# Six RMS normalisations in a three-block transformer kernel: rows scaled on VectorE and transposed, in place of products with a diagonal matrix

## The chip, the cores and the metric

The kernel runs on one NeuronCore of one Trainium2 chip. The metric is the device time of one execution in microseconds; the kernel before takes 2475.67 us (median of three runs, 2475.46 to 2476.18).

## The reference

Three blocks in a row work on one sequence of 256 tokens with 1024 channels, all in float32. Each block has two layers or one, and every layer is a mixer (attention, convolution or a recurrence) or a feed-forward part behind an RMS norm:

```python
def rms_norm(x, g, eps=1e-6):
    xf = x.astype(jnp.float32)
    y = xf * lax.rsqrt(jnp.mean(xf * xf, axis=-1, keepdims=True) + eps)
    return (y * g.astype(jnp.float32)).astype(x.dtype)

# block 1, layer l = 0, 1
h = rms_norm(x, norm1_g[l]) * (1.0 + scale1) + shift1        # norms 0 and 2
...
x = x + (1.0 + gate1) * mixed
h2 = rms_norm(x, norm2_g[l]) * (1.0 + scale2) + shift2       # norms 1 and 3
x = x + (1.0 + gate2) * ((jax.nn.silu(f_gate) * f_up) @ w_ffn_out[l])
# block 2 has one layer: its norm is norm 4
# block 3, layer l = 0, 1
h = rms_norm_3(x, norm_mix[l])                               # norms 5 and 7
x = x + hybrid_mixer(h, ...)
h = rms_norm_3(x, norm_ffn[l])                               # norms 6 and 8
x = x + swiglu(h, ...) if l % 2 == 0 else x + moe_swiglu(h, ...)   # eight experts, top k
```

## The kernel before

The tokens lie in two tiles of 128 partitions (t = 0, 1), the stream `x` is [128, 2, 1024] in SBUF. Every weight is loaded in chunks of 128 x 2048 into six `raw` buffers by SyncE. ScalarE rounds a chunk to `head` (L693), VectorE makes `rest = raw - head` (L1147, `make_rest`), and TensorE does each product in three matmuls of the float32r parts (`three`, L2019 to L2021). The activations go the same way: `hT` (channels on partitions) is split into `hTh` by ScalarE (L710) and `hTl` by VectorE (L1275, `rest_turned`). Each engine runs a program written out by hand; the order of the work is the order of the calls in it, and `feed` puts the chunk work (L693, L1147) between the rest.

The nine norms are numbered 0 to 8 in the order in which they run. A norm must turn `x` (tokens on partitions) into `hT` (channels on partitions), scaled by 1/rms of each token. For each tile t:

- ScalarE squares and sums (L722) and takes the root (L751 or L743);
- VectorE, in `scale_diagonal`, takes the reciprocal (L1252) and makes a diagonal matrix `diag[:, t, :] = ident * r` (L1254);
- TensorE, in `turn_norm`, waits for `diag_ready` and makes eight products of a 128 x 128 block of `x` with `diag` (L2142), which transpose and scale at once, in two halves of four, each with a step on `norm_turned`;
- VectorE, in `evac_turned`, brings each half from PSUM to `hT` with the gain (and, in blocks 1 and 2, the shift) per channel: four operations of 128 x 128 (L1266) where there is a shift, one of 128 x 512 (L1262) where there is none. ScalarE and VectorE then split it (L710, L1275).

Norms 1, 3, 6 and 8 follow an output product of a mixer (`norm_of_product`): TensorE, in `linear_by_tiles`, does all of tile 0, half of tile 1, then `turn_norm(n, 0, ...)`, then the other half of tile 1. VectorE adds tile 0 to the stream, scales, evacuates, and then waits for the last product of tile 1 to add it (L1288/L1290 or L1285). Behind the second `scale_diagonal` it makes the rest of one more weight chunk (L1147) before it evacuates tile 1, except in norm 8. TensorE meanwhile begins the feed-forward part on tile 0 in `ffn`: the first chunk for tile 0, then `turn_norm(n, 1, x)`, the second chunk for tile 0 (which needs that L1147), then both for tile 1.

Norms 2 and 7 (and 4) follow a feed-forward part (`norm_of_ffn`): TensorE has nothing between the last product and the next mixer but the two `turn_norm`, and the mixer's first product needs `hTl` of three half tiles. Norm 8 is that of the mixture of experts; there VectorE also makes the normalised rows `xn = x * r * gain` (L1321, L1337), which the gather of the experts' tokens multiplies (L2411), and the router's logits (L2387) need `hT`.

`xn` is [128, 2, 1024] too. Norms 4 and 5 have it as the source of their products, since there x times a gain is normalised a second time.

## Time and profile before

| | |
|---|---|
| median of 3 runs | 2475.67 us |
| the profiled execution's own time | 2475.45 us |
| its span in the trace | 2473.6 us |
| TensorE busy | 2363.7 us (96%) |
| VectorE busy | 1942.6 us (79%) |
| ScalarE busy | 1419.4 us (57%) |
| mean granted TensorE clock | 0.984 |
| mean DMA rate | 264 GB/s |

Busy times are sums over the span. A matmul's duration in the trace holds its way through the pipeline, so that matmuls in a row overlap; the distance from start to start tells the rate. Times in the views of the timeline and of the stretches are microseconds from the span's start. "Idle before, releaser" is how long an engine stood before an instruction and what ended that.

### The profile page before, as it was taken

What the parts mean: (1) busy time and instruction counts of PE and PEld (TensorE: products, weight loads), DVE (VectorE), ACT (ScalarE), POOL (GpSimd) and SP (SyncE); (2) the same over time, 40 slices, a digit from 0 to 9 for tenths busy, and PEclk for the clock granted to TensorE, in tenths of its full rate; (3) what the DMA queues carried; (4) which work ended last, traced back from release to release, by engine and by line L of the source; (5) the groups of instructions that cost most, each with busy time, mean ns of one, the idle gap of its engine ahead of it and who ended that gap; (6) DMA issues with size and microseconds to landing.
All of it is one profiled execution on the core that took longest, in us unless ns stands there. A gap on an engine that the chain in (4) does not pass through costs nothing.

```text
span 2473.6 us, 29836 instructions
## 1 busy us (share of the span) xinstructions
PE 2363.7 (96%) x11895; PEld 1979.3 (80%) x11895; DVE 1942.6 (79%) x1866; ACT 1419.4 (57%) x1410; POOL 17.4 (1%) x33
## 2 busy tenths in 40 slices
PE   4988999998999899899999989999999999999998
PEld 4866788867888798798888978888888888888886
DVE  6998878787797656675445769898989898989897
ACT  2654433546443454455334547777777777777776
POOL 0000000000000000000000000000000000000000
PEclk9998999999999999899999999999999999999999
DMA  9556889444598445445555439999999999999996
GB/s 339 189 181 240 304 294 347 158 139 142 188 340 298 148 158 180 133 165 186 188 195 181 155 131 360 360 363 351 358 351 365 352 361 353 360 354 361 348 365 217
DMA packets 434768, 652.93 MB, mean 264 GB/s; under 512 B 20144, under 2 KB 323888, under 8 KB 434624
## 3 DMA queue, kind: packets, MB, share of 16 engines
q1 hardware_dynamic: 432592, 644.63, 75.3%
q0 software_dynamic: 2032, 6.33, 0.8%
q8 instruction: 97, 1.59, 0.3%
q14 instruction: 47, 0.39, 0.0%
HBM read 649.82 MB, written 1.05 MB: 263 GB/s over the span
## 4 chain that ended last, share of the span: by engine, by line
PE 89%; DVE 7%; ACT 2%; issue 1%; DMA 1%; SPq 0%; ACTq 0%; DVEq 0%
PE pair L2019 27%; PE pair L2021 26%; PE pair L2020 26%; PE pair L2054 2%; PE tb L2230 2%; DVE rest L1147 1%; PE pair L2411 1%; DVE aw L1516 1%; PE pair L2142 1%; DMA raw<-in_ada_w 1%; PE tb L2097 1%; DVE gat L1166 1%; DVE hT L1266 1%; ACT aw L722 0%; PE pair L2155 0%
## 5 line engine op out<-in xcount | busy, mean ns | idle before, releaser
L1147 DVE TENSOR_TENSOR rest<-raw,head 128x2048 fp32r<-128x2048 f32 x544 | 1245.0, 2291 | 295.6 <-ACT head L693 279.9
L693 ACT ACTIVATE head<-raw 128x2048 fp32r<-128x2048 f32 x544 | 1039.3, 1912 | 325.1 <-PE pair L2021 294.2
L2019 PE MATMUL pair<-head,hTh 128*128 128x512 f32 x1864 | 744.2, 399 | 6.3 <-issue 3.0
L2021 PE MATMUL pair<-head,hTl 128*128 128x512 f32 x1864 | 728.3, 391 | 0.0
L2020 PE MATMUL pair<-rest,hTh 128*128 128x512 f32 x1864 | 727.3, 390 | 0.0
L2019 PEld LDWEIGHTS pair<-head,hTh 128*128 128x128 f32 x1864 | 350.8, 188 | 79.6 <-issue 9.1
L2021 PEld LDWEIGHTS pair<-head,hTl 128*128 128x128 f32 x1864 | 350.3, 188 | 74.4
L2020 PEld LDWEIGHTS pair<-rest,hTh 128*128 128x128 f32 x1864 | 351.1, 188 | 69.4 <-issue 1.2
L2019 PE MATMUL pair<-head,aTh 128*128 128x512 f32 x776 | 308.4, 397 | 4.0 <-issue 2.9
L2020 PE MATMUL pair<-rest,aTh 128*128 128x512 f32 x776 | 303.7, 391 | 0.0
L2021 PE MATMUL pair<-head,aTl 128*128 128x512 f32 x776 | 303.7, 391 | 0.0
L2019 PE MATMUL pair<-hTh,head 128*128 128x256 f32 x736 | 211.3, 287 | 15.4 <-issue 7.2
L2020 PE MATMUL pair<-hTl,head 128*128 128x256 f32 x736 | 209.9, 285 | 0.0
L2021 PE MATMUL pair<-hTh,rest 128*128 128x256 f32 x736 | 209.8, 285 | 0.0
L928 ACT ACTIVATE aTh<-tb 128x256 fp32r<-128x256 f32 (+1 forms) x145 | 62.8, 433 | 231.3 <-PE tb L2230 231.3
L2019 PEld LDWEIGHTS pair<-head,aTh 128*128 128x128 f32 x776 | 146.6, 189 | 38.5 <-issue 9.1
L2021 PEld LDWEIGHTS pair<-head,aTl 128*128 128x128 f32 x776 | 146.6, 189 | 31.2
L2020 PEld LDWEIGHTS pair<-rest,aTh 128*128 128x128 f32 x776 | 146.8, 189 | 30.5 <-issue 1.0
L924 ACT ACTIVATE qkv<-pair 128x256 f32<-128x256 f32 (+1 forms) x148 | 64.6, 436 | 174.8 <-PE pair L2021 174.8
L2019 PEld LDWEIGHTS pair<-hTh,head 128*128 128x128 f32 x736 | 143.0, 194 | 17.0 <-issue 8.8
L2020 PEld LDWEIGHTS pair<-hTl,head 128*128 128x128 f32 x736 | 143.1, 194 | 0.1
L2021 PEld LDWEIGHTS pair<-hTh,rest 128*128 128x128 f32 x736 | 142.9, 194 | 0.0
(302 smaller groups left out, 1637.8 us busy)
## 6 DMA issues: line engine op xcount, KB each, us to landing
raw<-in_moe_w_gate SPq DMA_DIRECT2D x224, 512.0 KB, 5.2
raw<-in_moe_w_up SPq DMA_DIRECT2D x224, 512.0 KB, 7.2
raw<-in_moe_w_down SPq DMA_DIRECT2D x224, 512.0 KB, 5.6
raw<-in_w_in SPq DMA_DIRECT2D x152, 512.0 KB, 4.6
raw<-in_ada_w SPq DMA_DIRECT2D x96, 512.0 KB, 5.5
raw<-in_w_ffn_in SPq DMA_DIRECT2D x88, 512.0 KB, 5.3
raw<-in_w_ffn_out SPq DMA_DIRECT2D x44, 512.0 KB, 5.4
raw<-in_w_out SPq DMA_DIRECT2D x40, 512.0 KB, 4.3
```

The costliest lines, as they stand in the source:

```text
L693: act.activation(head[:, c.split, :], raw[:, c.raw, :], ACT.Copy).then_inc(heads_done, 1)
L924: act.activation(sg[:, 0:nt, :], src, ACT.Silu).then_inc(sem("silu_ready"), 1)
L928: act.activation(aTh[:, :, 0:nt * P], tb[0][:, :].rearrange("p (k s) -> p k s", k=2)[:, :, 0:nt * P], ACT.Copy).then_inc(ath_ready, 1)
L1147: dve.tensor_tensor(rest[:, c.split, :], raw[:, c.raw, :], head[:, c.split, :].bitcast(F32), ALU.subtract).then_inc(rests_done, 1)
L1166: ins = dve.scalar_tensor_tensor(out=acc, in0=src, scalar=c_, in1=acc, op0=ALU.mult, op1=ALU.add)
L1266: ins = dve.tensor_scalar(hT[:, k, toks], ps[:, i, :], scale[:, k:k + 1], shift[:, k:k + 1], ALU.mult, ALU.add)
L1516: did(dve.scalar_tensor_tensor(out=conv[:, g, :], in0=upad[:, g, k:k + S], scalar=w_, in1=conv[:, g, :], op0=ALU.mult, op1=ALU.add))
L2019: pe.matmul(out_, lh, rh, start=start, stop=False, skip_group_check=True)
L2020: pe.matmul(out_, lh, rl, start=False, stop=False, skip_group_check=True)
L2021: return pe.matmul(out_, ll, rh, start=False, stop=stop, skip_group_check=True)
L2054: ins = pe.matmul(ps[:, t, :], hT[:, kk, toks], raw[:, c.raw, wcols], start=first, stop=last, skip_group_check=True)
L2230: ins = pe.transpose(tb[0][:, k * S + t * P:k * S + (t + 1) * P], act_[:, t, k * P:(k + 1) * P], ident)
```

## The change

The norms 1, 2, 3, 6, 7 and 8 (`TURNED`) no longer use the diagonal matrix; 0, 4 and 5 (`DIAGONAL`) do so as before. In the six, VectorE multiplies the rows of `x` by the reciprocal, in two halves of 128 x 512, into `xn`, with a step on `rows_scaled` for each half, and TensorE transposes the blocks of `xn` against the identity. In norm 8 the scaling takes the gain in as well, so that it also makes the rows for the gather; the evacuation there is then a plain copy, and TensorE's wait for `xn_ready` ahead of the gather goes.

```diff
+        DIAGONAL, TURNED = (0, 4, 5), (1, 2, 3, 6, 7, 8)
...
-            def scale_diagonal(t, squared=None):
+            def scale_rows(n, t, squared=None):
...
                 did(dve.reciprocal(r, r))
                 now()
-                dve.tensor_scalar(diag[:, t, :], ident, r, None, ALU.mult).then_inc(sem("diag_ready"), 1)
+                if n in DIAGONAL:
+                    dve.tensor_scalar(diag[:, t, :], ident, r, None, ALU.mult).then_inc(sem("diag_ready"), 1)
+                    return
+                for half in range(2):
+                    cols = slice(half * NT, (half + 1) * NT)
+                    if n == 8:
+                        dve.wait_ge(sem("gain_landed"), 16)
+                        ins = dve.scalar_tensor_tensor(out=xn[:, t, cols], in0=x[:, t, cols], scalar=r, in1=gain[:, cols],
+                                                       op0=ALU.mult, op1=ALU.mult)
+                    else:
+                        ins = dve.tensor_scalar(xn[:, t, cols], x[:, t, cols], r, None, ALU.mult)
+                    ins.then_inc(sem("rows_scaled"), 1)
 
             def evac_turned(n, t, half, scale, shift):
...
+                if n == 8:
+                    dve.tensor_copy(hT[:, ks, toks], ps).then_inc(sem("hT_ready"), 1)
+                    return
...
-                scale_diagonal(0, None if g is None else base + 6)
+                scale_rows(n, 0, None if g is None else base + 6)
                 tally["squared"] += 4 * per
-                if n == 8:
-                    dve.wait_ge(sem("gain_landed"), 16)
-                    dve.scalar_tensor_tensor(out=xn[:, 0, :], in0=x[:, 0, :], scalar=rstd[:, 0:1], in1=gain,
-                                             op0=ALU.mult, op1=ALU.mult).then_inc(sem("xn_ready"), 1)
...
-                scale_diagonal(1, None if g is None else base + 8)
-                if n == 8:
-                    dve.scalar_tensor_tensor(out=xn[:, 1, :], in0=x[:, 1, :], scalar=rstd[:, 1:2], in1=gain,
-                                             op0=ALU.mult, op1=ALU.mult).then_inc(sem("xn_ready"), 1)
+                scale_rows(n, 1, None if g is None else base + 8)
...
             def turn_norm(n, t, src):
 
                 free(f"norm{n}.{t}")
-                pe.wait_ge(sem("diag_ready"), 2 * n + t + 1)
+                if n in DIAGONAL:
+                    pe.wait_ge(sem("diag_ready"), 2 * DIAGONAL.index(n) + t + 1)
                 for half in range(2):
+                    if n in TURNED:
+                        pe.wait_ge(sem("rows_scaled"), 4 * TURNED.index(n) + 2 * t + half + 1)
                     for i in range(4):
                         cols = slice((4 * half + i) * P, (4 * half + i + 1) * P)
+                        if n in TURNED:
+                            ins = pe.transpose(bank(f"norm{n}.{t}")[:, half, i * P:(i + 1) * P], xn[:, t, cols], ident)
+                            continue
                         ins = pe.matmul(bank(f"norm{n}.{t}")[:, half, i * P:(i + 1) * P], src[:, t, cols], diag[:, t, :], start=True, stop=True)
                     ins.then_inc(sem("norm_turned"), 1)
...
-            pe.wait_ge(sem("xn_ready"), 2)
```

Nothing else moves. Three places on VectorE show it. The first is norm 2, between the first addition of tile 1 and the end of the norm; before (L1252 the reciprocal, L1254 the diagonal, L1266 the evacuation, L1275 the rest of `hT`):

```order
L1252 RECIPROCAL sm<-sm 128x1
L1254 TENSOR_SCALAR diag<-cst,sm 128x128
L1288 TENSOR_TENSOR gat<-pair,gbc 128x512
L1290 TENSOR_TENSOR x<-x,gat 128x512
L1235 TENSOR_SCALAR sm<-sm 128x1
L1266 TENSOR_SCALAR hT<-pair,sm 128x128 x4
L1252 RECIPROCAL sm<-sm 128x1
L1254 TENSOR_SCALAR diag<-cst,sm 128x128
L1266 TENSOR_SCALAR hT<-pair,sm 128x128 x8
L1275 TENSOR_TENSOR hTl<-hT,hTh 128x4x128 x3
```

The same place now (L1265 is the scaling, L1281 the evacuation, L1290 the rest of `hT`):

```order
L1253 RECIPROCAL sm<-sm 128x1
L1265 TENSOR_SCALAR xn<-x,sm 128x512 x2
L1303 TENSOR_TENSOR gat<-pair,gbc 128x512
L1305 TENSOR_TENSOR x<-x,gat 128x512
L1236 TENSOR_SCALAR sm<-sm 128x1
L1281 TENSOR_SCALAR hT<-pair,sm 128x128 x4
L1253 RECIPROCAL sm<-sm 128x1
L1265 TENSOR_SCALAR xn<-x,sm 128x512 x2
L1281 TENSOR_SCALAR hT<-pair,sm 128x128 x8
L1290 TENSOR_TENSOR hTl<-hT,hTh 128x4x128 x3
```

Two operations of 128 x 512 stand where one of 128 x 128 stood, ahead of the second addition and ahead of the evacuation of the second half tile.

The second place is tile 1 of norm 3, now (norms 1 and 6 read alike; before, L1254 stood in the place of L1265, and L1147 is L1148 here):

```order
L1290 TENSOR_TENSOR hTl<-hT,hTh 128x4x128
L1253 RECIPROCAL sm<-sm 128x1
L1265 TENSOR_SCALAR xn<-x,sm 128x512 x2
L1148 TENSOR_TENSOR rest<-raw,head 128x2048
L1281 TENSOR_SCALAR hT<-pair,sm 128x128 x8
```

The rest of the weight chunk stands behind the two scalings.

The third place is tile 1 of norm 8, before:

```order
L1252 RECIPROCAL sm<-sm 128x1
L1254 TENSOR_SCALAR diag<-cst,sm 128x128
L1337 SCALAR_TENSOR_TENSOR xn<-x,sm,gbc 128x1024
L1262 TENSOR_TENSOR hT<-pair,prm 128x4x128 x2
L1851 COPY sm<-tb 128x16
```

and now:

```order
L1253 RECIPROCAL sm<-sm 128x1
L1262 SCALAR_TENSOR_TENSOR xn<-x,sm,gbc 128x512 x2
L1274 COPY hT<-pair 128x4x128 x2
L1859 COPY sm<-tb 128x16
```

The diagonal is gone, and the one operation over 1024 columns is two over 512, which TensorE now waits for.

## Rows read from the trace of the kernel before

**Rows 1.** The page: busy times, and the chain that ended last, by engine.
```profile
PE 2363.7 (96%) x11895; PEld 1979.3 (80%) x11895; DVE 1942.6 (79%) x1866; ACT 1419.4 (57%) x1410; POOL 17.4 (1%) x33
PE 89%; DVE 7%; ACT 2%; issue 1%; DMA 1%; SPq 0%; ACTq 0%; DVEq 0%
```

**Rows 2.** Groups by line: busy us, mean ns | idle before, releaser.
```profile
L2142 PE MATMUL pair<-diag,x 128*128 128x128 f32 x224 | 30.6, 295 | 7.0 <-DVE diag L1254 7.0
...
L1254 DVE TENSOR_SCALAR diag<-cst,sm 128x128 f32<-128x128 f32 x18 | 5.2, 287 | 0.6
...
L1359 DVE TENSOR_SCALAR x<-xn,sm 128x1024 f32<-128x1024 f32 x4 | 2.8, 752 | 0.1
```

**Rows 3.** Timeline, TensorE, a transpose step of the first feed-forward part: start, us.
```profile
267.45 0.60 PE L2230 MATMUL tb<-cst,qkv 128*128 128x128 f32 x4
```

**Rows 4.** Timeline of norm 2: start, us, engine, line [idle before <-releaser].
```profile
447.26 0.29 DVE L1254 TENSOR_SCALAR diag<-cst,sm 128x128 f32<-128x128 f32 x1
...
447.69 2.02 PE L2142 MATMUL pair<-diag,x 128*128 128x128 f32 x16 [0.97 <-DVE diag L1254]
...
448.86 1.37 DVE L1266 TENSOR_SCALAR hT<-pair,sm 128x128 f32<-128x128 f32 x4
...
450.54 2.77 DVE L1266 TENSOR_SCALAR hT<-pair,sm 128x128 f32<-128x128 f32 x8
...
450.77 2.02 PE L2142 MATMUL pair<-diag,x 128*128 128x128 f32 x16 [1.05 <-DVE diag L1254]
...
453.22 1.89 DVE L1275 TENSOR_TENSOR hTl<-hT,hTh 128x512 fp32r<-128x512 f32 x3
...
455.21 0.36 PE L2019 MATMUL pair<-hTh,head 128*128 128x256 f32 x1 [2.42 <-issue]
```

**Rows 5.** Timeline of norm 7: two evacuations, and TensorE's next product.
```profile
1366.42 0.68 DVE L1262 TENSOR_TENSOR hT<-pair,prm 128x512 f32<-128x512 f32 x1
...
1367.82 0.69 DVE L1262 TENSOR_TENSOR hT<-pair,prm 128x512 f32<-128x512 f32 x1 [0.72 <-PE pair L2142]
...
1370.41 0.36 PE L2019 MATMUL pair<-hTh,head 128*128 128x256 f32 x1 [1.74 <-issue]
```

**Rows 6.** Timeline of norm 3: tile 0's products, and tile 1's end.
```profile
630.54 2.02 PE L2142 MATMUL pair<-diag,x 128*128 128x128 f32 x16 [0.55 <-DVE diag L1254]
...
635.34 0.69 DVE L1288 TENSOR_TENSOR gat<-pair,gbc 128x512 f32<-128x512 f32 x1 [0.39 <-PE pair L2021]
...
638.33 2.28 DVE L1147 TENSOR_TENSOR rest<-raw,head 128x2048 fp32r<-128x2048 f32 x1
...
640.76 0.47 PE L2019 MATMUL pair<-head,hTh 128*128 128x512 f32 x1 [0.18 <-DVE rest L1147]
```

**Rows 7.** Timeline of norm 8, VectorE on tile 1.
```profile
1457.26 0.69 DVE L1285 TENSOR_TENSOR x<-x,pair 128x512 f32<-128x512 f32 x1 [2.04 <-PE pair L2021]
...
1459.52 1.28 DVE L1337 SCALAR_TENSOR_TENSOR xn<-x,sm,gbc 128x1024 f32<-128x1024 f32 x1
...
1461.81 0.69 DVE L1262 TENSOR_TENSOR hT<-pair,prm 128x512 f32<-128x512 f32 x1 [0.20 <-PE pair L2142]
```

**Rows 8.** Stretches: us, busy (x) of PE, PEld, DVE, ACT, POOL, granted clock, DMA share, GB/s.
```profile
447.00:455.20 8.20, 4.04 (x32) 3.75 (x33) 8.06 (x24) 3.63 (x8) 0.53 (x1) 1.00 0.17 65
...
1037.70:1041.40 3.70, 3.67 (x17) 3.70 (x18) 2.25 (x5) 1.59 (x3) 1.16 (x2) 0.50 0.34 133
1041.40:1044.00 2.60, 2.60 (x24) 2.60 (x24) 1.88 (x1) 0.69 (x1) 2.31 (x4) 1.00 0.73 214
...
204.00:208.50 4.50, 0.47 (x4) 0.47 (x5) 4.47 (x4) 0.00 (x0) 0.00 (x0) 1.00 1.02 372
208.50:218.80 10.30, 4.73 (x19) 3.94 (x18) 7.65 (x6) 3.70 (x4) 0.00 (x0) 0.50 0.85 294
...
242.70:246.10 3.40, 3.40 (x13) 3.00 (x12) 3.17 (x9) 1.04 (x2) 0.00 (x0) 0.50 0.00 0
```

**Rows 9.** Timeline, TensorE, eight transposes ahead of the first output product.
```profile
215.14 1.97 PE L2132 MATMUL pair<-cst,gat 128*128 128x128 f32 x8 [5.57 <-DVE gat L1601]
```

More of the change, by code:

```diff
@@ L1381, in norm_of_ffn @@
                 add(1, 0)
-                scale_diagonal(0, None if g is None else base + 4)
+                scale_rows(n, 0, None if g is None else base + 4)
                 add(1, 1)
@@ L1385, in norm_of_ffn @@
                 evac_turned(n, 0, 0, scale, shift)
-                scale_diagonal(1, None if g is None else base + 8)
+                scale_rows(n, 1, None if g is None else base + 8)
                 tally["squared"] += 4 * per
@@ L1401, in norm_of_input @@
                 for t in range(T):
-                    scale_diagonal(t)
+                    scale_rows(0, t)
                 tally["squared"] += 2
```

## The prediction, made before the changed kernel had run

> **What bounds the kernel now.** I read the page first: TensorE is busy for 96% of the span and holds 89% of the chain that ended last, VectorE 7% [rows 1]. So time is lost or won only where TensorE stands, or where its own work shrinks. The groups by line come next: the products with the diagonal are records of 295 ns with only 7.0 us of waiting for `diag` in front of them [rows 2]. The timelines of norms 2, 7, 3 and 8 then tell what ends TensorE's pauses around these products, which differs from norm to norm [rows 4 to 7], and the stretches give TensorE's granted clock there [rows 8]. Times are set against the profiled execution, 2475.45 us, which lies 0.22 us under the median of the runs. A difference under 0.2% (5.0 us) is about what a measurement of this kernel can't tell from none.
>
> **The change on TensorE.** A tile's eight products are 16 records in 2.02 us [rows 4]. Without the last record's 0.28 that is 15 steps of 0.116 us, about 0.22 us for a product and 1.8 us for a tile. Four transposes take 0.60 us, the last record 0.27 of it [rows 3]: 0.11 us each, 0.9 us for a tile. Over 12 tiles TensorE is spared 12 x 0.9 = 10.6 us. Few of them lie where TensorE ends a wait.
>
> **The change on VectorE.** The diagonal takes 287 ns over 128 columns, a scaling of the same kind 752 ns over 1024 [rows 2]. On the line between them 512 columns take 0.49 us. Operations in a row overlap by about 0.09 us (the x4 in 1.37 us and the x8 in 2.77 us [rows 4] are 0.35 us apart), so a tile's two scalings hold VectorE for 0.8 us where the diagonal held it for 0.2: **0.6 us more per tile**. The first half is ready 0.2 us later than the diagonal was, the second 0.4 us behind it, which is as long as TensorE needs for the first half's four transposes, 0.44 us.
>
> **Norm 2.** VectorE works without a pause from the first diagonal at 447.26 to the three rests that end at 455.11, and TensorE's next product starts 0.1 us behind them [rows 4]. TensorE's two sets of products end long before they are needed: the second evacuation, of eight, follows on the reciprocal at once. So the saved 1.8 us are worth nothing here, and both scalings lie on the path: 2 x 0.6 = **+1.2 us**. Its bounds are +0.6 (if one of the two finds a gap) and +1.4.
>
> **Norm 7.** It evacuates in one operation per half, so VectorE does have gaps: at 1367.82 it had waited 0.72 us for TensorE's products [rows 5]. I place the new order in time. The first scalings push the addition of tile 1 by 0.6 us, and ScalarE's sum and root with it; the second reciprocal waited for the evacuation until now and so comes only 0.45 later. Its first half is ready 0.65 later than the diagonal was, TensorE then needs 0.44 instead of 0.9 us for it, and the evacuation of tile 1 starts about 0.25 us later. **+0.3 us**, between -0.2 and +1.2 (nothing hidden, as in norm 2).
>
> **Norms 1, 3 and 6.** Tile 0 stands in the stream of products: TensorE waits 0.55 us for the diagonal and then works on it [rows 6]. Now it begins 0.2 later and is done 0.9 earlier: -0.7 us. VectorE was waiting for TensorE's last product of tile 1 when it added it at 635.34 [rows 6], so the gain reaches ScalarE's root and the second reciprocal. There the two scalings take 0.6 us of it back, ahead of the chunk's rest (L1147). TensorE's wait behind the second tile's products ends with that rest, 0.18 us after the products themselves [rows 6]: shorter transposes only make this wait longer. What is left is -0.1 us each, **-0.3 us** in all; bounds -2.1 (the rest not in the way) and +0.3.
>
> **Norm 8.** No chunk's rest stands behind the second scaling. The operation over 1024 columns takes 1.28 us [rows 7], over 512 I take 0.69, as the additions of that width take [rows 7]. From the reciprocal on, the second half is scaled after 1.29 us, transposed after 1.87 and can be evacuated after 2.14; before it was after 2.49 (1461.81 against 1459.32). That is -0.35 us for a tile, and both tiles are on the path, since VectorE waited 2.04 us for TensorE in between [rows 7]: **-0.7 us**, bounds -1.2 and +0.3. The gain is no longer applied in the evacuation; it is a copy of the same width, at the same price. The wait for `xn_ready` that goes had long been satisfied.
>
> Without the clock that makes +1.2 + 0.3 - 0.3 - 0.7 = +0.5 us.
>
> **The clock.** In norm 2 TensorE is busy for 4.04 of 8.20 us, nearly all of it with the diagonal, and the granted clock stays at 1.00, the 2.4 GHz level [rows 8]. With transposes half of that busy time goes and the 8.2 us grow by 1.2 to some 9.4: 1.8 us of transposes in two pieces, and nothing else. The nearest rows: after 4.05 us of idling and the first four transposes, from 204.00 to 208.50, the clock fell to 0.50, the 1.2 GHz level, for 10.3 us [rows 8]. In norm 1 it fell for 3.4 us even with the diagonal there, behind a run of one-column products [rows 8]. So I expect a fall in norm 2, and in norm 7, where the pause is shorter but as empty. What it costs is shown where the same work started at 1037.7 with a low clock: 17 records in 3.70 us, and then, at 1.00, 24 in 2.60 [rows 8]. Half of the 3.7 us is lost: 1.8 us. The clock can also stay low for shorter or longer; 0 and 3.4 us are my bounds for each. Twice 1.8 is **+3.6 us**. TensorE holds 89% of the chain [rows 1], and behind either norm begin the mixer's first products, which wait for nothing else; so I count it in full.
>
> In norms 1, 3 and 6 TensorE's second visit to the norm is now 1.8 us of products and about 0.7 us of idling (some 0.5 before them, as at tile 0, and 0.18 behind [rows 6]). It becomes some 3.1 us with 0.9 us of transposes: it begins 0.7 us earlier and ends 0.1 earlier. That is close to where the clock falls, and I take one fall in the three, at the shortest spell shown: half of 3.4 us [rows 8], **+1.6 us**; bounds 0 and 4.8.
>
> A rule of the Trainium skill speaks to this. TensorE: Matmul & The Clock Gate, Part 4 (PE-mode transpose), says that the full clock "doesn't engage" for transposes, since they don't count as TensorE being busy. By it the three product norms would all fall. The trace agrees only in part: of the eight transposes at 215.14 the first stand in a spell at half clock [rows 9], and that spell ended at 218.8, only 2.0 us after the float32r products had resumed, whereas those at 1037.7 needed 3.7 us [rows 8].
>
> Sum: 0.5 + 3.6 + 1.6 = +5.7 us, **2481.2 us**.
>
> **The rivals.**
> - *The clock holds.* The transposes, or the products at either side, are enough. For it: the clock stood at 1.00 through norm 2's 8.2 us at half load [rows 8]. Against it: 204.00 to 208.50. Then +0.5 us: 2476.0 us, no change that can be told. Chance 0.22.
> - *The clock falls in all of the five.* For it: the 3.1 us in norms 1, 3 and 6 come near the 4.5 us at 204.00, and if transposes do not count nothing is in them. Two more falls of 1.6 us, and longer ones in norms 2 and 7 (2.5 us each): 2481.2 + 3.2 + 1.4 = 2485.8 us. Chance 0.20. This is the case of the skill's rule.
> - *Faster.* The chunk's rest (L1147) is not what TensorE waits for once everything shifts: it already ended only 0.18 us after the products [rows 6]. If VectorE's scalings cost under 0.3 us a tile more, the 0.7 us of tile 0 stay in norms 1, 3 and 6, tile 1 keeps some 0.5, and norm 2 costs 0.5: -3.6 + 0.5 - 0.3 - 0.7 = -4.1 us, and with no fall of the clock 2471.3 us. It needs both; the point is a scaling of 512 columns within about 0.35 us. Chance 0.07, a little over half of it beyond -5.0 us, should norm 1's fall of the clock [rows 8] go as well.
> - *The forecast*: 0.51.
>
> **How the numbers follow.** The forecast's case spreads by 2 us to either side for the clock's luck; two thirds of it lie beyond +5.0 us (0.35), the rest within (0.16). Slower: 0.35 + 0.20 = 0.55. Faster: 0.04 of the 0.07. Same: 0.16 + 0.22 + 0.03 = 0.41. The range leaves out the faster case, the low edge of the case in which the clock holds, and the upper half of the five falls: 2475.0 to 2486.0 us.
>
> **What would show it.** In the profile after: 24 scalings at about 0.49 us, four of them in norm 8 at 0.69, and 96 transposes with starts 0.11 us apart. Norm 2: VectorE without a pause, TensorE's first product 1.2 us later behind the same rests. Norms 1, 3 and 6: a longer wait for the rest L1147 (now L1148), about 1.7 us. Clock: stretches at 0.50 in norms 2 and 7 that reach some 4 us into the next product. If the clock stays at 1.00 there, the larger part of the sum is wrong; if TensorE resumes earlier in norms 1, 3 and 6, the account of the rest is.

## The result and the profile after

The changed kernel takes 2481.71 us, the median of 17 runs (2479.66 to 2488.59), against 2476.36 us for the kernel before (17 runs, 2474.30 to 2478.41). The ratio is 1.0021, with a 95% interval of 1.0015 to 1.0028: slower by 5.4 us. The profiled execution of the changed kernel is its slowest, 2488.59 us, 6.9 us over the median. Its own steps can be read; its total cannot, so a second profiled execution of the same kernel (from the run e0_after, 2482.83 us) stands beside it where the clock matters. One run of the whole study, in e11, took 4239 us at a mean granted clock of 0.696 and is left out of every median.

The page, against [rows 1]: busy times, and the chain that ended last.

```profile
PE 2367.2 (95%) x11799; PEld 1980.9 (80%) x11799; DVE 1948.1 (78%) x1876; ACT 1419.2 (57%) x1410; POOL 17.6 (1%) x33
PE 89%; DVE 7%; ACT 2%; issue 1%; DMA 1%; SPq 0%; DVEq 0%; ACTq 0%
```

TensorE has 96 records less (12 tiles, 16 records before, 8 now) and yet is busy 3.5 us longer. Fewer records and yet more busy time: the clock must have been lower somewhere, and the mean granted clock is 0.977 where it was 0.984. VectorE is busy 5.5 us longer.

The groups by line, against [rows 2] (busy us, mean ns of one | idle before, releaser):

```profile
L2154 PE MATMUL pair<-cst,xn 128*128 128x128 f32 x96 | 14.7, 301 | 11.4 <-DVE xn L1265 9.4 <-DVE xn L1262 2.0
...
L1265 DVE TENSOR_SCALAR xn<-x,sm 128x512 f32<-128x512 f32 x20 | 8.8, 484 | 0.4
...
L1262 DVE SCALAR_TENSOR_TENSOR xn<-x,sm,gbc 128x512 f32<-128x512 f32 x4 | 2.8, 750 | 0.1
```

The 20 scalings at 0.484 us are what the line between the widths had given (0.49). The four of norm 8 take 0.75, not 0.69. The transposes' mean of 301 ns is a mixture: their median is 273 ns, and those at the half clock take up to 448.

The timeline of norm 2, against [rows 4] (start, us, engine, line [idle before <-releaser]):

```profile
449.80 0.88 DVE L1265 TENSOR_SCALAR xn<-x,sm 128x512 f32<-128x512 f32 x2
...
450.44 1.06 PE L2154 MATMUL pair<-cst,xn 128*128 128x128 f32 x8 [1.17 <-DVE xn L1265]
...
453.46 0.88 DVE L1265 TENSOR_SCALAR xn<-x,sm 128x512 f32<-128x512 f32 x2
...
454.09 1.94 PE L2154 MATMUL pair<-cst,xn 128*128 128x128 f32 x8 [2.59 <-DVE xn L1265]
454.26 2.64 DVE L1281 TENSOR_SCALAR hT<-pair,sm 128x128 f32<-128x128 f32 x8
456.81 1.89 DVE L1290 TENSOR_TENSOR hTl<-hT,hTh 128x512 fp32r<-128x512 f32 x3
...
458.80 0.55 PE L2027 MATMUL pair<-hTh,head 128*128 128x256 f32 x1 [2.77 <-issue]
```

VectorE works without a pause from 449.80 to the rests of `hT`. TensorE's next product starts 9.00 us after the first scaling; before it was 7.95 us after the first diagonal [rows 4]. That is +1.05 us. The second tile's eight transposes take 1.94 us where the first tile's took 1.06: the clock had fallen between them, and the next product, 0.55 instead of 0.36 us, finds it low.

Norm 3, tile 1, against [rows 6]:

```profile
645.07 1.06 PE L2154 MATMUL pair<-cst,xn 128*128 128x128 f32 x8 [0.30 <-DVE xn L1265]
645.23 2.29 DVE L1148 TENSOR_TENSOR rest<-raw,head 128x2048 fp32r<-128x2048 f32 x1
...
647.66 0.47 PE L2027 MATMUL pair<-head,hTh 128*128 128x512 f32 x1 [1.53 <-DVE rest L1148]
```

TensorE's wait for the chunk's rest has grown from 0.18 to 1.53 us, in the place where the transposes got shorter.

Norm 7, against [rows 5], and norm 8's second tile, against [rows 7]:

```profile
1374.89 0.88 DVE L1265 TENSOR_SCALAR xn<-x,sm 128x512 f32<-128x512 f32 x2
...
1375.69 1.28 DVE L1277 TENSOR_TENSOR hT<-pair,prm 128x512 f32<-128x512 f32 x2
...
1378.87 0.55 PE L2027 MATMUL pair<-hTh,head 128*128 128x256 f32 x1 [2.29 <-issue]
```
```profile
1469.76 0.16 DVE L1253 RECIPROCAL sm<-sm 128x1 f32<-128x1 f32 x1 [1.18 <-ACT sm L752]
...
1470.85 1.94 PE L2154 MATMUL pair<-cst,xn 128*128 128x128 f32 x8 [1.76 <-DVE xn L1262]
...
1472.58 4.27 PE L2401 MATMUL tb<-trig,hT 128*128 128x8 f32 x20
```

In norm 7 two evacuations, the second half of tile 0 and the first of tile 1, stood apart before and now run in one piece: VectorE's gap of 0.72 us [rows 5] is used up. The last row, in norm 8, is of the router's products. In the trace of before they took 2.30 us:

```profile
1461.61 2.30 PE L2387 MATMUL tb<-trig,hT 128*128 128x8 f32 x20
```

The stretches, against [rows 8] (us, busy (x) of PE, PEld, DVE, ACT, POOL, granted clock, DMA share, GB/s). First the kernel before behind norm 8, then the changed kernel's norm 2, norm 7, norm 1, the product ahead of norm 3, and norm 8:

```profile
1464.60:1474.90 10.30, 6.99 (x32) 6.91 (x33) 6.91 (x24) 0.80 (x2) 0.00 (x0) 0.50 0.13 46
```
```profile
452.70:462.90 10.20, 6.04 (x27) 5.70 (x28) 9.47 (x23) 4.68 (x7) 0.68 (x1) 0.50 0.15 55
1377.70:1384.40 6.70, 5.53 (x26) 5.56 (x27) 6.00 (x6) 2.43 (x2) 0.00 (x0) 0.50 0.05 6
254.90:258.30 3.40, 3.40 (x9) 2.63 (x9) 3.30 (x9) 1.79 (x3) 0.17 (x1) 0.52 0.75 211
616.80:620.20 3.40, 3.40 (x10) 2.67 (x9) 2.06 (x2) 2.53 (x2) 0.00 (x0) 0.53 0.00 0
1469.90:1486.50 16.60, 11.73 (x54) 11.56 (x55) 9.84 (x32) 1.92 (x3) 0.00 (x0) 0.50 0.01 2
```

Norms 2 and 7 have a spell (a stretch at one low clock) at 0.50, the 1.2 GHz level, that the trace of before does not have. So has norm 1, beside its old one [rows 8]. The one ahead of norm 3 lies in a stream of products that the change does not touch. The spell at norm 8 was there before, but it began 5.5 us behind the second reciprocal and lasted 10.3 us, where it now begins 0.1 us behind and lasts over 16.6. The second profiled execution of the changed kernel separates what belongs to the change from what belongs to that one execution:

```profile
449.20:459.60 10.40, 6.01 (x27) 5.67 (x28) 9.67 (x23) 4.92 (x8) 0.67 (x1) 0.51 0.14 54
1374.20:1382.00 7.80, 6.44 (x34) 6.47 (x35) 6.95 (x7) 2.55 (x3) 0.00 (x0) 0.56 0.13 29
251.20:254.40 3.20, 2.83 (x7) 2.29 (x8) 3.20 (x10) 1.02 (x2) 0.00 (x0) 0.50 0.51 130
613.00:616.50 3.50, 3.50 (x10) 2.73 (x9) 1.76 (x2) 2.90 (x3) 0.00 (x0) 0.51 0.00 0
640.00:648.00 8.00, 6.09 (x29) 4.41 (x29) 7.52 (x15) 2.63 (x6) 0.31 (x1) 1.00 0.36 129
1131.00:1140.00 9.00, 7.45 (x37) 5.85 (x36) 7.27 (x11) 4.06 (x6) 0.00 (x0) 1.00 0.32 117
```

Norms 2, 7 and 1 fall again. (Behind norm 8 the spell began 3.5 us after the second reciprocal this time, at 1469.8, and ended at 1480.0.) Norms 3 and 6 stay at 1.00, here as in the first profile. The spell ahead of norm 3 is there again, at 613.0. It is not the change's: the profiles of e5 and e8 below, with the diagonal in norms 1 to 3, have it too, and from norm 2's first reciprocal to norm 3's it costs 1.6 us (184.46 us in e5, 182.84 in the kernel before, whose profile lacks it).

One more wait has changed, and it lies at the very end, in the last norm: VectorE's mean (L1235, now L1236), ScalarE's root of it (L751, now L752), and VectorE's reciprocal of that (L2004, now L2012). First before, then in the changed kernel:

```profile
2465.45 0.17 DVE L1235 TENSOR_SCALAR sm<-sm 128x2 f32<-128x2 f32 x1
...
2466.01 0.29 ACT L751 ACTIVATE sm<-sm 128x1 f32<-128x1 f32 x1
...
2467.63 0.16 DVE L2004 RECIPROCAL sm<-sm 128x1 f32<-128x1 f32 x1 [2.02 <-ACT sm L751]
```
```profile
2480.16 0.17 DVE L1236 TENSOR_SCALAR sm<-sm 128x2 f32<-128x2 f32 x1 [2.39 <-issue]
2480.36 0.29 ACT L752 ACTIVATE sm<-sm 128x1 f32<-128x1 f32 x1 [1.99 <-DVE sm L1236]
...
2480.76 0.16 DVE L2012 RECIPROCAL sm<-sm 128x1 f32<-128x1 f32 x1 [0.44 <-ACT sm L752]
```

In the changed kernel VectorE stands for 2.39 us ahead of the mean and waits for nothing that the profile shows. In the kernel before it stands too, one operation later. The profile puts those 2.02 us down to ScalarE's root, but that root had ended at 2466.30, 1.33 us before the reciprocal began, and the gain vector that VectorE also waits for there was loaded at 1040.2; in the changed kernel the reciprocal begins 0.11 us behind the root. So the wait is not new. It has moved ahead of the operation that ScalarE's root needs, and less of it is hidden: from the last four updates of `x` to the last scaling of the result it is 6.63 us before (2462.60 to 2469.23) and 7.30 now (2475.05 to 2482.35), so **+0.7 us**.

### The profile page after: what moved, and what is told of

Its sections match the earlier page's. It is cut to its first block, busy times and chain, and to the rows that moved or that the text cites. A ratio compares the mean times of both kernels' runs of the same rounds, so it can differ in the third digit from the quotient of the medians.

```text
span 2486.7 us, 29655 instructions
## 1 busy us (share of the span) xinstructions
PE 2367.2 (95%) x11799; PEld 1980.9 (80%) x11799; DVE 1948.1 (78%) x1876; ACT 1419.2 (57%) x1410; POOL 17.6 (1%) x33
## 3 DMA queue, kind: packets, MB, share of 16 engines
HBM read 649.82 MB, written 1.05 MB: 262 GB/s over the span
## 4 chain that ended last, share of the span: by engine, by line
PE 89%; DVE 7%; ACT 2%; issue 1%; DMA 1%; SPq 0%; DVEq 0%; ACTq 0%
PE pair L2027 27%; PE pair L2029 26%; PE pair L2028 26%; PE pair L2062 2%; PE tb L2244 2%; PE pair L2424 1%; DVE aw L1524 1%; DVE rest L1148 1%; DMA raw<-in_ada_w 1%; PE tb L2105 1%; DVE gat L1167 1%; ACT aw L723 1%; DVE hT L1281 0%; PE pair L2156 0%; PE pair L2169 0%
## 5 line engine op out<-in xcount | busy, mean ns | idle before, releaser
L1148 DVE TENSOR_TENSOR rest<-raw,head 128x2048 fp32r<-128x2048 f32 x544 | 1245.2, 2291 | 304.2 <-ACT head L694 288.6
L2027 PE MATMUL pair<-hTh,head 128*128 128x256 f32 x736 | 214.8, 292 | 15.7 <-issue 8.1
```

The costliest lines, as they stand in the source:

```text
L1148: dve.tensor_tensor(rest[:, c.split, :], raw[:, c.raw, :], head[:, c.split, :].bitcast(F32), ALU.subtract).then_inc(rests_done, 1)
L2027: pe.matmul(out_, lh, rh, start=start, stop=False, skip_group_check=True)
```

## The experiments

In the kernels below the tuple TURNED names the norms that are scaled by halves and transposed, DIAGONAL those that keep the diagonal. Where norm 8 keeps it, its rows for the gather are made as before, and TensorE's wait for `xn_ready` is back. `keep_busy(n)` issues n products of the identity with itself into a bank of `tb` that holds nothing wanted at that moment; they keep TensorE occupied and change no result. Differences in us are between the medians of two kernels' runs, and the interval is that of the ratio, which weighs all the runs; the two can differ by 0.7 us.

**e0_after: the changed kernel once more.**

> The changed kernel again, as the yardstick for its neighbours. Clock theory (the transposes leave TensorE's pauses in norms 2 and 7 nearly empty, the granted clock falls there, and VectorE's scalings add 1.2 us in norm 2 and 0.3 in norm 7): 5 us over the kernel before, with 0.50 stretches in norms 2 and 7 of the profile. Rival (VectorE only: every tile's 0.6 us of scaling lands on the path, the clock plays no part): 5 to 7 us over, and the stretches where the clock is low are those of the kernel before.

Measured: 2482.41 us (8 runs, 2479.84 to 2485.34), ratio 1.0022 [1.0012, 1.0033]. The stretches above are its own. The loss is in the kernel, not in one unlucky execution; what that execution had on top was longer spells (at norm 4 13.7 us in place of two of 3.4, behind norm 8 17.1 in place of 10.2).

**e3_only_2_7: norms 2 and 7 alone.**

```
-        DIAGONAL, TURNED = (0, 4, 5), (1, 2, 3, 6, 7, 8)
+        DIAGONAL, TURNED = (0, 1, 3, 4, 5, 6, 8), (2, 7)
```

> Only norms 2 and 7 are scaled and transposed; 1, 3, 6 and 8 have the diagonal again. Clock theory: 1.5 us of VectorE and two falls of the clock at 1.8 us, so 5.1 us over the kernel before (3 to 7 by the length of the falls), low stretches in norms 2 and 7. Rival (VectorE only): at most 4 tiles x 0.6 = 2.4 us over.

Measured: 2482.96 us (10 runs), ratio 1.0023 [1.0014, 1.0033], +5.9 us. Both norms have their spell (450.0 to 460.2 and 1375.0 to 1381.8), and norm 1 shows only the one that the kernel before has. Two of the six norms are enough for a loss as large as the whole change's. (In this profile the spell at norm 4 lasts 17.1 us against 10.2 in the kernel before, which costs 3.4 us from norm 4 to norm 5 and has nothing to do with the edit.)

**e1_identity_2_7: scaled by halves, but plain products with the identity in place of transposes.** The other norms keep the diagonal.

```
-                            ins = pe.transpose(bank(...)[:, half, i * P:(i + 1) * P], xn[:, t, cols], ident)
+                            ins = pe.matmul(bank(...)[:, half, i * P:(i + 1) * P], xn[:, t, cols], ident, ...)
```

> As the kernel with only norms 2 and 7 changed, but TensorE multiplies the scaled rows with the identity as a plain product (two records each, 0.22 us) and does not transpose. VectorE's work is the same, TensorE's busy time in the pauses is that of the kernel before. Clock theory: the clock stays at 1.00 in norms 2 and 7, only VectorE's 1.2 us in norm 2 and some 0.8 in norm 7 (the slower half product is waited for) are left: 2.0 us over the kernel before, so 3 us under the one that transposes. Rival (VectorE only): the same time as the one that transposes, or 0.4 us more.

Measured: 2479.15 us (11 runs, 2476.25 to 2483.42), ratio 1.0010 [1.0001, 1.0019], +2.1 us. With TensorE's full work of products back, over half of e3's loss is gone in the medians, although VectorE's work is that of e3. Four of its runs lie at 2476.3 to 2476.8, four at 2483.2 to 2483.4 and three between, and the profile is one of the upper four (2483.31): norm 2 has a spell of 3.4 us in it, norm 7 none. (Most of what sets this execution apart lies elsewhere, in spells of 17.1 us at norm 4 and behind norm 8.) The mean granted clock of the runs says the same of the rest: it is 0.985 in the four fastest, a level that some runs of the kernel before reach and none of e3 does (0.979 to 0.981 in all ten). So the products do not hold the clock reliably, but with them it falls less.

**e2_keep_busy_2_7: the changed kernel, with idle products behind the transposes of norms 2 and 7.**

```
                     turn_norm(n + 1, t, src)
+                    keep_busy({(2, 0): 8, (2, 1): 12, (7, 0): 8, (7, 1): 8}.get((n + 1, t), 0))
```

> The changed kernel with products of the identity with itself, into a PSUM tile that nobody reads then, put into TensorE's pauses: in norm 2 eight behind the first tile's transposes and twelve behind the second's, in norm 7 eight and eight (0.22 us each, shorter than the pauses). They compute nothing that is used. Clock theory: the clock stays at 1.00 in both norms and the time is 3.6 us under the changed kernel, 1.5 us over the kernel before. Rival (VectorE only): no gain over the changed kernel.

Measured: 2479.53 us (11 runs, 2478.36 to 2481.01), ratio 1.0014 [1.0005, 1.0023]: 2.9 us under e0_after, which ran on the same chip. The two stretches around norm 2 and norm 7, in the same columns as above:

```profile
446.00:462.00 16.00, 13.06 (x106) 12.23 (x105) 15.10 (x34) 7.01 (x14) 0.68 (x1) 1.00 0.09 35
1369.00:1383.00 14.00, 13.49 (x114) 13.17 (x113) 11.38 (x13) 6.21 (x7) 0.00 (x0) 1.00 0.32 107
```

The clock is 1.00 in both. This is the changed kernel with no other difference than what TensorE does while it waits, so the 2.9 us are the price of the falls in norms 2 and 7. The runs of the two kernels overlap (2479.84 to 2485.34 and 2478.36 to 2481.01), so this figure is uncertain by over 1 us. The profiles give the price with less chance in it. From a norm's first reciprocal on VectorE to the next norm's, in us:

| profile | norm 2 to 3 | norm 7 to 8 |
|---|---|---|
| before | 182.84 | 88.21 |
| changed kernel, first profile | 187.33, the spell ahead of norm 3 in it | 90.92 |
| e0_after | 187.19, the same | 90.83 |
| e3 | 186.05 | 90.74 |
| e1 | 185.39, a spell of 3.4 us at norm 2 | 88.83 |
| e2 | 183.91 | 88.44 |

With the clock held (e2) norm 2 costs 1.07 us more than before and norm 7 0.23: VectorE's part. From e2 to e3 the falls add 2.14 and 2.30 us, and to the two profiles of the changed kernel, less 1.6 for the spell ahead of norm 3, 1.7 to 1.8 and 2.4 to 2.5. So the two falls cost 4.1 to 4.4 us in the profiled executions, where 3.6 had been forecast.

**e4_only_1_3_6 and e5_only_8**: TURNED is (1, 3, 6) and (8,).

> Only norms 1, 3 and 6 are scaled and transposed. My account (tile 0's 0.7 us is given back ahead of the chunk's rest, and the clock falls once more, in norm 1, where it also fell in both profiles of the changed kernel): -0.3 + 1.6 = 1.3 us over the kernel before, and in the timeline a wait of some 1.7 us for the rest L1148 behind the second tile's transposes. Rival (TensorE's shorter work counts in full): 6 tiles x 0.9 = 5 us under it. Rival (VectorE's 0.6 us a tile in full): 3.6 us over it.

> Only norm 8 is scaled with its gain and transposed. My account: 0.35 us a tile, 0.7 us under the kernel before, which the times alone can hardly show; in the trace the copy of the second tile's second half comes 2.1 us after the reciprocal's end where it came after 2.5. Rival: the longer scaling in front of the first transposes costs more than they give back, no change or 0.8 us over.

Measured: e4 2478.22 us, ratio 1.0006 [0.9997, 1.0015], +1.9 us; e5 2477.34 us, ratio 1.0005 [0.9995, 1.0014], +1.0 us (11 runs each). Neither interval leaves out zero. The traces say more. In e4 one of the three norms has a new spell, norm 1, and norms 3 and 6 have none:

```profile
252.30:255.70 3.40, 3.19 (x8) 2.54 (x9) 3.30 (x11) 1.38 (x3) 0.00 (x0) 0.50 0.57 152
```

From norm 1's first reciprocal to norm 2's it is 207.10 us in e4 and 206.18 before, so with the spell norm 1 costs 0.9 us. In e5 the spell begins 2.1 us behind norm 8's second reciprocal, and the router's products run at half clock as in the changed kernel's first profile:

```profile
1459.32 4.27 PE L2405 MATMUL tb<-trig,hT 128*128 128x8 f32 x20
```

But the profile of e1, which has the diagonal in norm 8, shows the same (its spell begins 1.5 us behind the second reciprocal, and the 20 products take 4.27 us). So an early fall there does not need norm 8's edit. The three parts, 5.9, 1.9 and 1.0 us, add up to 8.8, the whole is 5.4. Each has an interval of over 2 us to either side, so this is no contradiction, but neither is it a proof that the parts add.

**e6_keep_busy_4_5 and e7_keep_busy_more: the diagonal kept but for norm 8, idle products in the pauses that the kernel always had.** Here the clock in norms 4 and 5 is the object (14 idle products ahead of norm 4's first tile, 8 and 4 around its second, 13, 18 and 4 around norm 5's tiles); e7 adds some in the second mixer layer, ahead of the router's ranks (10) and of the first gather (4).

> As the kernel with only norm 8 changed, and products of the identity with itself, whose output nobody reads, in TensorE's pauses of norms 4 and 5, where the kernel before has its clock at 0.50 for 10, 3 and 10 us. If the clock is what such pauses cost (clock theory): the diagonal's products take 2.0 us and not 3.75 for a tile, and the next products start at 1.00: -2.9 us in norm 4, -5.4 in norm 5, -0.7 in norm 8, 9 us under the kernel before. If the pauses' own waits decide (rival): 1 us under it at most.

> The same with idle products also ahead of the turned channels of layer 1 (ten), ahead of the router's ranks (ten) and ahead of the first gather (four). Clock theory: the gather's records, 6.3 us at 0.50 in the kernel before, take 3.5, and the products after the turned channels start at 1.00: another 4.5 us less than with norms 4 and 5 alone, 13 us under the kernel before. Rival: the extra products delay the ranks and the gather and nothing is won.

Measured: e6 2472.82 us, ratio 0.9983 [0.9974, 0.9992], -3.5 us; e7 2471.92 us, ratio 0.9983 [0.9974, 0.9992], -4.4 us. Both are faster than the kernel before, by less than half of what was expected (9 and 13 us). The kernel before at norms 4 and 5, then e6:

```profile
831.00:848.00 17.00, 11.12 (x62) 10.62 (x63) 14.38 (x41) 8.48 (x21) 0.00 (x0) 0.70 0.00 1
1018.00:1036.00 18.00, 9.74 (x45) 8.86 (x44) 9.87 (x20) 6.77 (x14) 0.00 (x0) 0.77 0.16 55
```
```profile
831.00:848.00 17.00, 14.14 (x120) 13.66 (x119) 15.28 (x40) 8.17 (x20) 0.88 (x2) 1.00 0.00 1
1016.00:1034.00 18.00, 15.44 (x119) 14.36 (x119) 11.87 (x24) 7.91 (x18) 0.00 (x0) 1.00 0.23 72
1452.80:1470.20 17.40, 12.08 (x55) 11.91 (x56) 10.33 (x32) 2.36 (x4) 0.00 (x0) 0.53 0.03 5
```

The clock rises from 0.70 and 0.77 to 1.00 as meant. From norm 4's first reciprocal to norm 6's the time went from 287.05 to 282.08 us: -5.0 where -8.3 had been forecast. Norm 4 gave 0.9 us and not 2.9 (VectorE, not TensorE, decides it, as in norm 2), and norm 5 gave 4.1 and not 5.4. And 2.6 of these 5.0 us were lost again from norm 8's first reciprocal on: 2.1 between the second reciprocal and the last updates of `x`, where the spell at half clock now lasts 17.1 us (it fills the last row but for its first 0.9 us), and 0.9 in the last norm, less 0.3 that norm 8 won. In e7 that spell lasts 6.8 us, and the same way to the end takes 2.9 us less than in e6, but from norm 2 to norm 3 e7 takes 1.6 us more, with the spell ahead of norm 3 that e6 happens not to have. The idle products in the second mixer layer gave nothing that shows.

**e8_before_keep_busy: the kernel before, diagonal everywhere, idle products in every long pause**: those of e7, and 5 ahead of norm 8's second tile.

> The kernel before (diagonal in all nine norms) with products of the identity with itself, whose output nobody reads, in TensorE's pauses: those of norms 4 and 5, ahead of the turned channels of layer 1, ahead of tile 1's products of norm 8 (five), ahead of the router's ranks (ten) and the first gather (four). Account after the last runs (the pauses of norms 4 and 5 gave 5 us in the trace, not 8.3, since VectorE decides in norm 4): 5 to 7 us under the kernel before. Rival (what was won in the last two kernels came from norm 8's transposes, not from the clock): 4 us or less, under what they won.

Measured: **2469.00 us** (7 runs, 2466.96 to 2470.68), ratio 0.9969 [0.9958, 0.9980], -7.6 us, more than the 5 to 7 expected. Its stretches through norms 5 and 8 (norm 4 reads as in e6):

```profile
1018.00:1036.00 18.00, 15.44 (x121) 14.43 (x120) 11.87 (x25) 7.74 (x17) 0.00 (x0) 1.00 0.24 78
1453.00:1468.00 15.00, 14.32 (x123) 13.74 (x122) 10.52 (x33) 3.10 (x6) 0.00 (x0) 1.00 0.00 1
```

The kernel before had a clock of 0.50 from behind the router's products nearly to the end of the gather. This kernel is faster than both that the study began with, and it has no transposes in any of the nine norms, so the gain of e6 and e7 was not that of norm 8's edit.

**e9_after_keep_busy: the changed kernel with the same, and idle products behind the transposes too** (norms 2 and 7 as in e2, 6 behind the second tile of norms 1, 3 and 6, 3 behind norm 8's).

> The changed kernel with the same idle products, and with those of norms 2 and 7, six behind the second tile's transposes in norms 1, 3 and 6, and three behind norm 8's. So the clock is held up in both kernels of this pair and their difference is that of VectorE's and TensorE's own work. Account: +1.2 in norm 2, +0.3 in norm 7, -0.1 each in norms 1, 3 and 6, -0.7 in norm 8, 0.5 us over its neighbour (-0.5 to +1.5). Rival (VectorE's 0.6 us a tile lands on the path in most norms): 4 us or more over it.

Measured: 2472.38 us (11 runs, 2469.12 to 2474.39), ratio 0.9981 [0.9972, 0.9990], 3.4 us over e8 where 0.5 was expected. Even with the clock cared for everywhere, the change does not pay. From the two traces: norm 2 takes 1.03 us longer (forecast 1.2) and norm 7, up to norm 8's first reciprocal, 0.24 (0.3). From norm 1's first reciprocal to norm 2's it is 1.4 us, with a fall of the clock from 240.7 to 244.1 that e8 does not have. That fall is not the change's: the kernel before has it in the same place [rows 8], e8 happens to lack it, and from norm 0's first reciprocal to norm 1's e9 takes 1.2 us less than e8, whose spell ahead of norm 1 is 3.4 us longer. Behind norm 8's second reciprocal it is 1.9 us. Of these, 0.4 to 0.5 are there at the first expert's chunks and stay so over all the experts; 1.4 arise in the last 23 us, where the wait without a visible cause stands ahead of the mean in e9. In e8 it stands one operation later, as in the kernel before: the reciprocal begins at 2461.20, 1.59 us after its root had ended.

```profile
2463.13 0.17 DVE L1236 TENSOR_SCALAR sm<-sm 128x2 f32<-128x2 f32 x1 [3.33 <-issue]
```
```profile
2458.76 0.17 DVE L1236 TENSOR_SCALAR sm<-sm 128x2 f32<-128x2 f32 x1
```

**e10_busy_only_8 and e11_busy_only_1_3_6: e8 with norm 8 alone turned, and with norms 1, 3 and 6 alone** (6 idle products behind each second tile). They were to tell whether e9's surplus was theirs.

> The kernel with idle products in every long pause (diagonal everywhere), with norm 8 alone turned into scaling and transposes. The step between it and e8_before_keep_busy is what norm 8's edit costs when the clock does not fall around it. By my sum: -0.7 us (-1.2 to +0.3), 2468.3 us against 2469.0. Rival one: norm 8's edit costs some 1.6 us even so, 2470.6 us or more, because the eight transposes count for less activity than sixteen product records and the clock falls after them; then the profile shows the router's 20 products in over 4 us and the half level behind the second tile's transposes. Rival two: the 1.6 us that e9_after_keep_busy lost after norm 8 were a product of its own clock in the expert part; then nothing of it shows here. Where the clock holds, VectorE's second reciprocal of norm 8 should come 0.35 us sooner after the first than in e8 and the first expert product a further 0.35 us sooner.

> The same kernel with idle products in every long pause, with norms 1, 3 and 6 alone turned, and six idle products behind each one's second tile. My terms: -0.3 us, 2468.7 us against 2469.0 of e8_before_keep_busy, as long as the clock does not fall in them. Rival: one fall, in norm 1, that the idle products do not prevent (e9_after_keep_busy lost 1.4 us between the reciprocals of norm 1 and norm 2 with a fall from 240.7 to 244.9): 2470.1 to 2470.5 us. Rival two: the three norms cost over 3 us together, which would say that e9's loss was theirs and not that of norms 2 and 8.

Measured: e10 2468.44 us (6 runs), ratio 0.9968 [0.9957, 0.9980], -0.6 us against e8; e11 2469.42 us (6 runs), ratio 0.9969 [0.9958, 0.9981], +0.4 us. Norm 8's second tile in e8, then in e10:

```profile
1455.11 0.16 DVE L1253 RECIPROCAL sm<-sm 128x1 f32<-128x1 f32 x1 [1.18 <-ACT sm L752]
...
1457.60 2.30 PE L2416 MATMUL tb<-trig,hT 128*128 128x8 f32 x20
```
```profile
1453.58 0.16 DVE L1253 RECIPROCAL sm<-sm 128x1 f32<-128x1 f32 x1 [1.18 <-ACT sm L752]
...
1454.67 1.23 PE L2165 MATMUL pair<-cst,xn 128*128 128x128 f32 x8 [0.54 <-DVE xn L1266]
...
1455.74 2.30 PE L2416 MATMUL tb<-trig,hT 128*128 128x8 f32 x20
```

From the reciprocal to the router's products it is 2.49 us in e8 and 2.16 in e10: -0.33. From norm 8's first reciprocal to its second, 7.33 and 6.98: -0.35. So at the full clock norm 8's edit is worth the 0.7 us that the sum gave it. The clock fell at 1459.1, 5.5 us behind the second reciprocal and behind the router's products, for 3.4 us. The landmarks show this, not the total of -0.6, in which such terms can't be told from chance. In e11 norm 1's first reciprocal to norm 2's is 204.45 us against 204.60, norm 3 to norm 4 203.65 against 203.80, norm 6 to norm 7 242.76 against 242.88: each -0.1, as the sum had it, and no fall of the clock in norm 1 this time. Behind norm 8's second reciprocal, where e11 and e8 are the same code, e11 took 1013.3 us to the end against 1012.0: it had a fall of the clock there that e8 had not (the stretch, same columns),

```profile
1460.40:1463.80 3.40, 3.40 (x20) 3.40 (x19) 1.72 (x10) 0.20 (x1) 0.00 (x0) 0.55 0.00 0
```

and the wait ahead of the mean, 2.39 us, as e10 had it with 2.45. It stands there in 12 of the 14 profiles, 2.3 to 3.3 us long. The two that have it one operation later, with 2.02 and 2.27 us, are the kernel before and e8, the only ones with the diagonal in all nine norms. From the last updates of `x` to the last scaling the twelve take 7.2 to 8.2 us, the two 6.6 and 6.9.

## Why the prediction was right

The forecast of 2481.2 us (range 2475.0 to 2486.0) stands against 2481.71 us, and its likeliest sign, slower by over 0.2%, is the one that came: 0.21%, at the very edge of what can be told. Against the rivals: "the clock holds" (+0.5 us) lies outside the interval, and e2 and e3 show the clock's share; "falls in all five" (+10.4) does too, and norms 3 and 6 stayed at 1.00 in both profiles; "faster" needed a scaling within 0.35 us, which took 0.48. Point by point:

- **The prices.** Scaling of 512 columns 0.49 forecast, 0.484 measured; two in a row 0.88 us, which is the 0.49 twice less the overlap of 0.09; eight transposes in 1.06 us, steps of 0.11 as forecast. Only norm 8's own scaling was off, 0.75 for 0.69; the additions of that width had been the wrong row to take it from.
- **Norm 2**, +1.2: 1.05 in the changed kernel, 1.07 in e2, 1.03 in e9 against e8. VectorE was without a pause and TensorE's saving was worth nothing, as stated.
- **Norm 7**, +0.3: 0.23 in e2, 0.24 in e9 against e8. The second reciprocal came 0.44 us later against the first than before, placed at 0.45.
- **Norms 1, 3 and 6**, -0.1 each: -0.12 to -0.15 each in e11. The saving of tile 0 is there (the second reciprocal comes 0.76 us sooner in norm 1 and 0.73 in norm 6, forecast 0.7), is given back by tile 1's scalings, and what TensorE saves on tile 1 turns into its wait for the chunk's rest: 1.53 us, forecast 1.7.
- **The clock in norms 2 and 7**, +3.6: both fell, and TensorE's next products ran 4.1 us (norm 2) and 5.5 us (norm 7) at half level before it rose. The medians of e0_after and e2 put the price at 2.9 us, the profiles at 4.1 to 4.4: 1.7 to 2.1 for norm 2, as forecast, and 2.3 to 2.5 for norm 7, where 1.8 had been too little.
- **One fall in norms 1, 3 and 6**, +1.6: one, norm 1's, in both profiles of the changed kernel, in e2 and in e4. With it norm 1 took 0.9 to 1.05 us more than before, so the fall cost 1.0 to 1.2. Norm 1 was the one with an old spell beside it [rows 8]. That it was this one was not forecast.
- **Norm 8**, -0.7: this step was incomplete. The sum is right at the full clock (e10). In the changed kernel's first profile, and in e5, the clock falls 0.1 and 2.1 us behind the second reciprocal instead of 5.5, and the router's 20 products take 4.27 us instead of 2.30. In the second profile it fell in the midst of those products (3.12 us). Whether the edit brings this about is not shown, since e1, with the diagonal in norm 8, has it too. The forecast looked for falls in the five norms whose next work is a stream of products, and its working for norm 8 never looks at the clock. What the term comes to is open: e5 gives +1.0 us with an interval from -1.2 to +3.5, and from the second reciprocal to the last record of the gather it is 16.5 us before, 18.3 in the changed kernel's first profile and 15.7 in its second.
- **A term that the sum did not have**: the wait in the last norm, +0.7 us in the changed kernel's first profile and +0.9 in its second. With it, and with the falls in norms 2 and 7 at 4.1 to 4.4 us, the terms read from the profiles (without norm 8's) add up to about 7 us, against 5.4 for the medians. Beside them single executions differ by terms of the clock that are not the change's: 1.6 us for the spell ahead of norm 3, and up to 3.4 us for the length of the one at norm 4. So the mechanism stands, but that the total came within 0.5 us is in good part luck.

The Trainium skill's rule, TensorE: Matmul & The Clock Gate, Part 4 (PE-mode transpose), that transposes don't count as TensorE being busy the way products do, had stood for falls in all of the five. The traces agree with it in part. e1, in which only the kind of the operation differs from e3 at the same places, loses 3 to 4 us less (3.8 in the medians), but a plain product also takes twice the time of a transpose (0.22 against 0.11 us), so e1 does not tell the kind from the time. In norms 3 and 6, where only transposes stand in the pause, the clock held. No run here took kind and time apart.

## What to carry to other kernels

Before an operation of TensorE is made cheaper, look at what ends its wait there: if another engine does, the saving turns into a longer wait, and where the clock falls in the emptier pause, that can cost more than the saving was worth, in the work behind it. Where a pause can't be filled with work, products that nobody reads are a cheap cover: they took 7.6 us (0.3%) off this kernel (e8), with no change of its algorithm. Look for spells at half clock in the trace of the kernel as it is, before looking for operations to spare.

## What the runs showed of the chip that had not been expected

- A spell at half clock costs the small things too: 20 products of 128 x 8 took 4.27 us in it and 2.30 outside, and they lie on the path alone.
- A spell's place and length differ between executions of the same code. Behind norm 8 it lasted 17.1 us in e6, with norms 4 and 5 held at 1.00, but also in e1, with nothing filled, against 10.3 in the kernel before and none in e8. So e6 does not show that filling one pause lengthens a spell elsewhere.
- VectorE's wait of 2.0 to 3.3 us in the last norm. Nothing in the code near it differs between e8 and e9, and it stands one operation later only where the diagonal is in all nine norms, so its place goes with an edit far ahead of it; most likely one on VectorE, whose program has more instructions in the others. In all 14 the program has a jump over the loop for a second window right ahead of the mean, so the jump alone does not set the place. The Trainium skill, Runtime: NRT & Kernel Launch, Instruction fetch mechanics, has engines fetch instructions in blocks and calls the cost of a block's border mostly hidden; a border that has moved against the code might look like this. No run here was made to show it, so the cause stays open.
- Where identical code ran, the time of a stage still differed by the clock: from norm 4's reciprocal to norm 5's it is 187.7 us in e8 and e9 and 186.1 in e10 and e11. The row of e8 shows where, a fall in the midst of products without a pause, which e9 has too and e10 and e11 do not:

```profile
997.20:1000.60 3.40, 3.40 (x9) 2.67 (x10) 1.38 (x2) 3.17 (x3) 0.00 (x0) 0.54 0.00 0
```

A term of 1 us can be read from two profiles only where the clock of the stretch is looked at as well.
